# Reordering the first stage of a hybrid decoder layer: an earlier second chunk, eight buffers for modulation weights, squares summed by TensorE

## What is computed

```
mod = silu(c) @ w_ada + b_ada                      # c: one vector per sequence, 9 in all; w_ada: 1024 x 6144
sh1, sc1, gt1, sh2, sc2, gt2 = split(mod, 6)
h = rmsnorm(x, norm1_g) * (1.0 + sc1) + sh1        # rmsnorm: x * rsqrt(mean(x*x) + eps) * g
proj = h @ w_in                                    # then RG-LRU, mLSTM and pool groups, w_out, and the MLP
```

## Time and profile before

| what | value |
|---|---|
| median of 3 runs | 1172.3 us |
| the profiled execution | 1172.33 us |
| its span in the trace | 1170.5 us |
| PE busy | 1123.7 us, 96% of the span |
| DVE, ACT, POOL busy | 795.6, 470.4, 341.7 us |
| mean DMA rate over the span | 94 GB/s |
| start of `V:0` in the trace | 51.66 us |
| start of `V:5` in the trace | 93.79 us |

### The profile page before, as it was taken

One profiled execution on the slowest core, in us unless ns is written; L12 is line 12 of the kernel. 1 busy time (PEld: TensorE's weight loads), 2 busy tenths in 40 slices (PEclk: granted clock), 3 DMA queues, 4 the chain that ended last, 5 costly groups with the idle time before them and its releaser, 6 DMA issues.

```text
span 1170.5 us, 19691 instructions
## 1 busy us (share of the span) xinstructions
PE 1123.7 (96%) x7237; PEld 1075.4 (92%) x7237; DVE 795.6 (68%) x1327; ACT 470.4 (40%) x774; POOL 341.7 (29%) x273
## 2 busy tenths in 40 slices
PE   4899999999989999999999999999999999999997
PEld 2688888888978999899999999999999999999996
DVE  4472455489775434778678879778778787788546
ACT  5452355555456343642233332332432433433431
POOL 1133011201425357764022032122231231231352
PEclk9799999999989999999999999999999999999998
DMA  9812523566623822111111111202202102111104
GB/s 316 311 66 82 142 91 126 171 186 225 187 79 122 270 75 72 54 55 37 37 36 55 56 36 60 66 18 72 67 9 80 59 18 78 47 53 55 37 1 145
DMA packets 67846, 109.85 MB, mean 94 GB/s; under 512 B 6435, under 2 KB 42567, under 8 KB 67399
## 3 DMA queue, kind: packets, MB, share of 16 engines
q1 hardware_dynamic: 57574, 84.88, 21.9%
q10 hardware_dynamic: 10208, 24.12, 6.5%
HBM read 96.81 MB, written 12.18 MB: 93 GB/s over the span
## 4 chain that ended last, share of the span: by engine, by line
PE 81%; DVE 11%; ACT 3%; issue 1%; POOL 1%; DMA 1%; SPq 0%; ACTq 0%; POOLq 0%; DVEq 0%
PE D L2412 7%; PE D L2414 6%; PE D L2413 6%; PE D L2596 6%; PE D L2598 5%; PE D L2597 5%; PE X L2598 5%; PE X L2596 5%; PE X L2597 5%; PE X L2668 5%; PE X L2670 5%; PE X L2669 5%; PE D L2668 2%; PE D L2670 2%; PE D L2669 2%
## 5 line engine op out<-in xcount | busy, mean ns | idle before, releaser
L2412 PE MATMUL D<-H_hi,W_hi 128*128 128x344 f32 x472 | 159.1, 337 | 6.9 <-POOL H_lo L1086 6.1
L2414 PE MATMUL D<-H_hi,W_lo 128*128 128x344 f32 x472 | 152.1, 322 | 0.0
L2413 PE MATMUL D<-H_lo,W_hi 128*128 128x344 f32 x472 | 152.1, 322 | 0.0
L1086 POOL TENSOR_TENSOR Y_lo<-FU,Y_hi 128x344 fp32r<-128x344 f32 (+3 forms) x84 | 100.1, 1195 | 153.7 <-ACT Y_hi L1522 87.6
L1081 POOL TENSOR_TENSOR W_lo<-RAWW,W_hi 128x1024 fp32r<-128x1024 f32 x25 | 61.3, 2452 | 178.8 <-ACT W_hi L1235 178.5
L2412 PEld LDWEIGHTS D<-H_hi,W_hi 128*128 128x128 f32 x472 | 90.1, 191 | 17.7 <-issue 11.8
L1086 POOL TENSOR_TENSOR Y_lo<-EY,Y_hi 128x344 fp32r<-128x344 f32 (+1 forms) x24 | 38.3, 1597 | 216.3 <-ACT Y_hi L1522 144.5
L2413 PEld LDWEIGHTS D<-H_lo,W_hi 128*128 128x128 f32 x472 | 90.1, 191 | 0.6 <-issue 0.2
L2414 PEld LDWEIGHTS D<-H_hi,W_lo 128*128 128x128 f32 x472 | 89.8, 190 | 0.0
L2220 DVE SCALAR_TENSOR_TENSOR X<-X,MOD 128x344 f32<-128x344 f32 (+1 forms) x138 | 75.6, 566 | 9.3 <-PE X L2670 9.2
L2668 PE MATMUL X<-Y_hi,W_hi 128*128 128x344 f32 x252 | 80.7, 320 | 0.0
(11 more groups left out here) (417 smaller groups left out, 3434.8 us busy)
## 6 DMA issues: line engine op xcount, KB each, us to landing
RAWW<-in_W SPq DMA_DIRECT2D x76, 512.0 KB, 3.6
RAWW<-in_WADA ACTq DMA_DIRECT2D x28, 512.0 KB, 4.1
RAWW<-in_WADA SPq DMA_DIRECT2D x20, 512.0 KB, 6.5
RAWW<-in_W ACTq DMA_DIRECT2D x18, 512.0 KB, 3.7
X0T<-in_x SPq DMA_DIRECT2D x3, 1376.0 KB, 12.9
out_y<-OUTN SPq DMA_DIRECT2D x24, 172.0 KB
X<-in_x SPq DMA_DIRECT2D x8, 344.0 KB, 5.5
NM<-nm_d SPq DMA_DIRECT2D x8, 256.0 KB, 5.4
```

The costliest lines, as they stand in the source:

```text
L1086: nc.gpsimd.tensor_tensor(lo_v, fu_v, hi_v.bitcast(F32), ALU.subtract).then_inc(lo_ready, 1)
L2412: T.matmul(out, w_h, hi[:, kt, a:b], start=(kt == 0), stop=False)
L2413: T.matmul(out, w_h, lo[:, kt, a:b], start=False, stop=False)
L2414: one = T.matmul(out, w_l, hi[:, kt, a:b], start=False, stop=(kt == KT - 1))
```

## The change

Six things, all in the first stage:

- `x` chunk 1 is asked for behind the fourth piece (after `w0`) instead of behind the sixteenth, chunk 2 behind the sixteenth.
- The 16 starting pieces go to eight buffers: the four of `RAWW` and four spare places in memory that is free then (three where `WV_lo` will be, one in `MU`'s place). A piece waits for the use of the piece eight before it. Eight pieces leave the ring's numbering, so `R:20` becomes `R:12`, and so on.
- `MIX_ORDER` begins with the squares of chunk 0 instead of with pieces, and the squares and the norm of chunk 1 stand directly behind `N:0:0 N:0:1`.
- From there the two chunks go on together, row tile by row tile, with the units' products on chunk 1 between those on chunk 0. `DK:1:1` (unit 1 on chunk 1) stays whole and stands ahead of `V:0`.
- The squares of chunks 0 and 1 are no longer added by DVE. PE multiplies each square by the ones matrix and accumulates in the norm's bank: eight fp32 matmuls for a chunk instead of one. ACT waits for PE before it overwrites one of the two `SQ` tiles.
- The squares of chunk 2 are still added by DVE; they move from before `V:2` to between `V:0` and `V:1`, and `NS:2` to behind `V:1`.

```diff
-SP_AFTER = {5: ("w0",), 7: ("w1",), 15: ("wv", "x1"), 17: ("x2",), 18: ("w2",)}
+SPARE = 4
+SPARE_PIECES = [k for n, k in enumerate(ADA_EARLY) if n % (RAW + SPARE) >= RAW]
+SP_AFTER = {3: ("w0", "x1"), 5: ("w1",), 15: ("wv", "x2"), 17: ("w2",)}
 ...
-ADA:0:0 ADA:0:1 SQ:0:0 ADA:4:0 ADT:0 ADM:0 ADA:4:1 SQ:0:1 ADA:1:0 ADT:4 ADM:4 NS:0 ADA:1:1 W:0 N:0:0 N:0:1 ADA:5:0 ADT:1 ADM:1
-ADA:5:1 W:1 ADA:2:0 ADT:5 ADM:5 DK:0:0:0:2 N:0:2 N:0:3 ADA:2:1 DK:1:0:0:2 ADA:6:0 ADT:2 ADM:2 ADA:6:1 DK:0:0:2:4
-    ADA:3:0 ADT:6 ADM:6 N:0:4 N:0:5 DK:1:0:2:4 ADA:3:1 ADA:7:0 ADT:3 ADM:3 DK:0:0:4:6 ADA:7:1 ADT:7 ADM:7 N:0:6 N:0:7 DK:1:0:4:6
+SQ:0:0 ADA:0:0 SQ:0:1 NS:0 ADA:0:1 ADA:4:0 ADT:0 ADM:0 ADA:4:1 ADT:4 ADM:4 W:0 N:0:0 N:0:1
+SQ:1:0 SQ:1:1 ADA:1:0 DK:0:0:0:2 ADA:1:1 NS:1 ADA:5:0 ADT:1 ADM:1 W:1 ADA:5:1 DK:1:0:0:2 ADT:5 ADM:5 N:1:0 N:0:2 N:0:3 N:1:1
+ADA:2:0 ADA:2:1 DK:0:1:0:1 DK:0:0:2:3 ADA:6:0 ADT:2 ADM:2 DK:1:0:2:3 ADA:6:1 DK:0:0:3:4 DK:1:0:3:4 ADT:6 ADM:6 N:0:4 N:1:2 N:0:5 N:1:3
+DK:0:1:1:2 ADA:3:0 ADA:3:1 DK:0:1:2:3 ADA:7:0 DK:0:0:4:5 ADT:3 ADM:3 DK:1:0:4:5 ADA:7:1 DK:0:1:3:4 ADT:7 ADM:7 N:0:6 N:1:4 N:0:7 N:1:5 N:1:6 N:1:7
+DK:0:0:5:6 DK:1:0:5:6
 WV:0 DK:0:0:6:7
 ...
-D:0:0 SQ:1:0
-D:1:0 SQ:1:1 V:0 NS:1 ADA:8:0 N:1:0 N:1:1 V:1 N:1:2 N:1:3 DK:0:1:0:1
 ...
+WV:3 D:0:0 DK:0:1:5:6
+D:1:0 DK:0:1:6:7
+DK:0:1:7:8
+D:0:1 DK:1:1:0:8
+D:1:1 V:0 ADA:8:0 SQ:2:0 V:1 SQ:2:1 NS:2
+R:12 ADA:8:1 V:2 N:2:8 N:2:0 R:13 N:2:1 N:2:2 V:3 N:2:3 N:2:4 N:2:5 ADT:8 N:2:6 V:4 N:2:7 ADM:8 DK:0:2:0:8
 ...
+            def square_taken(n):
+
+                c, kt = n // KT, n % KT
+                if c >= N_PE_SQ:
+                    act.wait_ge(ss1_done, n - N_PE_SQ * KT + 1)
+                elif kt == KT - 1:
+                    wait_full(act, ("NS", c))
+                else:
+                    act.wait_ge(sq_summed, c * (KT - 1) + kt + 1)
 ...
+                    for kt in range(part * KT // 2, (part + 1) * KT // 2):
+                        n = c * KT + kt
+                        pe.wait_ge(sq_ready, n + 1)
+                        one = T.matmul(bank(key)[:, 0:CH], ONE[:], SQ[:, n % 2, :], start=(kt == 0), stop=(kt == KT - 1))
```

More of the change, by code:

```diff
@@ L54 @@
 ADA_START = (0, 4, 1, 5, 2, 6, 3, 7)
-ADA_FIRST = 2 * len(ADA_START)
+ADA_EARLY = [("ADA", i, h) for i in ADA_START for h in range(2)]
 N_MIX = 2 * LRU_T + 3 * ML_T + POOL_T
@@ L120 @@
 W:2 V:5
-D:0:2 R:22 DK:1:2:0:8
-ADA:9:0 ADA:9:1 R:23 V:6 V:7 W:3 V:8 R:25 ADT:9
+D:0:2 R:14 DK:1:2:0:8
+ADA:9:0 ADA:9:1 R:15 V:6 V:7 W:3 V:8 R:17 ADT:9
 D:1:2 ADM:9 ADA:10:0 G1 ADA:10:1
-D:2:0 ADT:10 R:24
-D:2:1 ADM:10 R:26 G2
-D:2:2 R:28 W:4 G3 ADA:11:0 R:27 R:29
+D:2:0 ADT:10 R:16
+D:2:1 ADM:10 R:18 G2
+D:2:2 R:20 W:4 G3 ADA:11:0 R:19 R:21
 D:3:0 ADA:11:1 G4
-D:3:1 R:31 ADT:11 LRUC:0
+D:3:1 R:23 ADT:11 LRUC:0
 D:3:2 ADM:11 W:5 ADA:12:0
-D:4:0 R:30 ADA:12:1 LRUG:0 R:32 LRUA:0
+D:4:0 R:22 ADA:12:1 LRUG:0 R:24 LRUA:0
@@ L131 @@
 D:4:1 LRUM:0
-D:4:2 R:34 W:6
-D:5:0 ADT:12 ADM:12 ADA:13:0 ADA:13:1 R:33 LRUC:1
+D:4:2 R:26 W:6
+D:5:0 ADT:12 ADM:12 ADA:13:0 ADA:13:1 R:25 LRUC:1
 D:5:1
-D:5:2 ADT:13 R:35 ADM:13 ADA:14:0 LRUG:1 ADA:14:1
-D:6:0 R:37 W:7 ADT:14 LRUA:1 R:36 R:38 ADM:14
+D:5:2 ADT:13 R:27 ADM:13 ADA:14:0 LRUG:1 ADA:14:1
+D:6:0 R:29 W:7 ADT:14 LRUA:1 R:28 R:30 ADM:14
 D:6:1 LRUM:1
-D:6:2 R:40 ADA:15:0
+D:6:2 R:32 ADA:15:0
 D:7:0
-D:7:1 W:8 ADA:15:1 LRUC:2 R:39
+D:7:1 W:8 ADA:15:1 LRUC:2 R:31
 D:7:2 ADT:15 LRUG:2 LRUA:2
-D:8:0 R:41 ADM:15 ADA:16:0 W:9
@@ L143 @@
-D:8:1 R:43
-D:8:2 R:42 ADA:16:1 R:44 W:10 LD:0 SMA TS TSD ADT:16 LRUM:2
+D:8:0 R:33 ADM:15 ADA:16:0 W:9
+D:8:1 R:35
+D:8:2 R:34 ADA:16:1 R:36 W:10 LD:0 SMA TS TSD ADT:16 LRUM:2
 D:9:0
-D:9:1 R:46 R:45 LD:1 ADM:16 EX:0 ADA:17:0 S:0 SX:0 ADA:17:1 W:11 AB:0 R:47
+D:9:1 R:38 R:37 LD:1 ADM:16 EX:0 ADA:17:0 S:0 SX:0 ADA:17:1 W:11 AB:0 R:39
 D:9:2 ADT:17 U:0 NU:0 HN:0 CN:0 ADM:17 HM:0 EX:1 ADA:18:0 SMK S:1 SX:1 SMB:0
@@ L173, in plan_mix @@
 def plan_mix():
-    raws = [("ADA", i, h) for i in ADA_START for h in range(2)]
+    raws = [k for k in ADA_EARLY if k not in SPARE_PIECES]
     pairs = [i for i in range(NPAIR) if i not in ADA_START]
     early, pairs = pairs[:2], pairs[2:]
-    raws += [("ADA", i, h) for i in early for h in range(2)]
+    early = [("ADA", i, h) for i in early for h in range(2)]
+    raws += early
     for u in range(3, N_MIX):
@@ L185, in plan_mix @@
         out.append((name, *(int(a) for a in args)))
-    return out, raws
+    return out, raws, ADA_EARLY + early
 AUX = ["X0", "X1", "X2", "X3", "X4"]
@@ L298, in build @@
     P_FF = P_MIX + P_NORM
-    assert len(raw_seq) == N_MIX - N_EARLY_W + NADA
+    assert len(raw_seq) == N_MIX + R0
     raw_seq += [("W", u) for u in range(N_MIX, N_MIX + RAW)]
     raw_at = {k: n for n, k in enumerate(raw_seq)}
-    ADA_ORDER = [k[1] for k in raw_seq if k[0] == "ADA" and k[2] == 0]
+    ADA_ORDER = list(ADA_START) + [k[1] for k in raw_seq if k[0] == "ADA" and k[2] == 0 and k[1] not in ADA_START]
     SHIFTED = ((1, 3, 5, 7, KT), (KT - 2, KT - 1, KT))
@@ L367, in build @@
         WV_lo = at("WV_lo", [P, KT, VCOLS], rX + KT * VCOLS * 4, F32R)
+        SPARE_RAW = [at(f"SPARE{r}", [P, KT * P], rX + KT * VCOLS * 4 + r * KT * P * 4 if r < SPARE - 1 else slot[15]) for r in range(SPARE)]
         VS = [at(f"VS{b}", [P, HEADS, HV], rX + 2 * KT * VCOLS * 4 + 1568 * b) for b in range(2)]
@@ L478, in build @@
         raw_in = [sem(f"raw{r}_in") for r in range(RAW)]
+        spare_in = [sem(f"spare{r}_in") for r in range(SPARE)]
         w_hi_ready, w_lo_ready = sem("w_hi_ready"), sem("w_lo_ready")
@@ L560, in load_raw, with used @@
                 e.dma_start(RAWW[:, n % RAW, :], I["W"][in_unit(u)]).then_inc(raw_in[n % RAW], 16)
[L562 to L564 removed]
+        def used(e, key):
             if key[0] == "W":
@@ L570, in raw_used @@
                 e.wait_ge(ada_half, ADA_ORDER.index(key[1]) + 1)
+        def raw_used(e, n):
+            used(e, raw_seq[n])
         def mod_ready(e):
@@ L809, in _ @@
             load_x(0)
[L810 to L813, removed]
+            for n, key in enumerate(sp_raws):
+                if key in SPARE_PIECES:
+                    k = SPARE_PIECES.index(key)
+                    if k >= SPARE:
+                        used(sp, SPARE_PIECES[k - SPARE])
+                    load_piece(sp, key, SPARE_RAW[k % SPARE][:], spare_in[k % SPARE])
+                else:
+                    if raw_at[key] >= RAW:
+                        raw_used(sp, raw_at[key] - RAW)
+                    load_raw(sp, raw_at[key])
                 for what in SP_AFTER.get(n, ()):
@@ L2422, in _ @@
                 k = s[0]
-                if k == "NS":
-                    sum_squares(s, s[1], ss1_done, (s[1] + 1) * KT)
+                if k == "SQ" and s[1] < N_PE_SQ:
+                    _, c, part = s
+                    key = ("NS", c)
+                    if part == 0:
+                        take(key)
+                    for kt in range(part * KT // 2, (part + 1) * KT // 2):
+                        n = c * KT + kt
+                        pe.wait_ge(sq_ready, n + 1)
+                        one = T.matmul(bank(key)[:, 0:CH], ONE[:], SQ[:, n % 2, :], start=(kt == 0), stop=(kt == KT - 1))
+                        if kt < KT - 1:
+                            one.then_inc(sq_summed, 1)
+                        else:
+                            done(one, key)
+                elif k == "NS" and s[1] >= N_PE_SQ:
+                    sum_squares(s, s[1], ss1_done, (s[1] + 1 - N_PE_SQ) * KT)
                 elif k == "ADA":
```

90 lines of the change are left out of this document (42 added, 48 removed).

## The result

The changed kernel takes 1193.6 us (median of 4 runs, 1191.78 to 1196.85) against 1172.59 for the kernel before in the same session (1172.24 to 1173.58). The ratio is 1.0177, 95% interval 1.0154 to 1.0200: 21 us slower. The prediction said slower, by 8.7 us, and 1181.0; the time lies outside its range of 1170 to 1186. The profiled execution took 1191.78 us, the shortest of the four, with a span of 1190.0 against 1170.5; so the traces differ by 19.5 us and the medians by 21.0.

A forecast was written before the change was run, and what follows sets the result against it. PE was taken as the bound, 96% busy. `V:5` at 101.1 plus 1.4 for the clock, against 93.79 before, gave 8.7 us more: 1181.0 us from 1172.33, range 1170 to 1186.

The forecast's parts named there:

- the walk to 43 us: First stage, queue by queue from the start until DVE starts `N:1:0`, put at 42.65 us against `N:0:6` at 44.58 before.
- rival *faster: Waits of 17.4 us in the first stage are covered: 1163.6 us if all, deciding from half; chance 0.19.
- I am wrong if: Signs: `N:1:0` starts below 36, PE isn't idle ahead of `SQ:1:0`, or the trace distance shrinks from `V:5` to the end.
- first batch: Unit 0 on chunk 1, from `N:1:0` at 42.65: 8.25 us, plus 1.4 for starting at half clock.
- `NS:2` to `V:5`: End of the walk: chunk 2's norm, pieces, `V` products and a `DK` of 3.8, from 82.8 to 101.1 us.
- until the rise some 4 us on, of which 0.45 fills the wait: +1.4: First batch starts at half clock, its `DK`s, piece and `ADT` costing 1.9 more, less 0.45 absorbed: 1.4 us.
- wait of 3 us ahead of `NS:2`: PE waits 3 us for DVE's second half of chunk 2's squares, which stands behind the copy of `V:1`.
- 8.25 us a batch: Each of the first two batches of chunk 1's pieces, from DVE's start through `ADM`, takes 8.25 us at full clock.
- 2.6 + 0.95: Head of each batch: 2.6 us from DVE's start until the first low part is there, 0.95 to the next.
- a bound of 0 to +2: Issue time of some 10 PE switches between a piece and a `DK`, left out of the walk: 0 to +2 us.
- every batch at half clock: Rival: waits of 2.3 and 2.0 us make batches two and three start low too, 1.5 to 2 each: 1184.5 us; chance 0.14.
- the distance should not have grown: Behind `V:5` both kernels have the same work left, so a shift there moves the end by about as much.

The follow-up runs named there:

- after_fill: Changed kernel with filler matmuls on PE, whose results nobody reads, ahead of its six long waits; 1191.99 us, ratio 1.0132.
- after_dve_order_fill: Changed kernel with all squares added by DVE, fillers on PE, chunk 2's squares ahead of `V:0` and the `D:0:0` copy moved earlier; 1175.54 us, ratio 1.0011.
- before_first_fill: Kernel before with eight buffers, chunk 0's squares first (on DVE), chunk 1 asked for behind the value weights, and fillers in an unused bank; 1169.66 us, ratio 0.9967.
- after_order: Changed kernel with chunk 2's squares ahead of `V:0` and the `D:0:0` copy ahead of the third value-weight part, no fillers; 1194.4 us, ratio 1.0168.
- after_dve_squares: Changed kernel with the squares of chunks 0 and 1 added by DVE again; 1193.2 us, ratio 1.0153.

## Why the prediction was right in sign and short in size

**Right: the walk to 43 us.** First sum 9.15 (said 9.75), first reciprocal ended 20.5 (21.2), PE idle 4.14 (4.4) ahead of chunk 1's first sum at 25.58 (26.45), second reciprocal ended 38.95 (39.15), 3.07 idle (3) on `W_lo`, `N:1:0` at 43.55 (42.65). Nothing hid PE's sums, the early chunk was no help, and eight buffers gave nothing that a time shows. Chunk 0's first four sums took 4.63 us and chunk 1's eight 7.80, half of them at half clock, about as walked (4.75 and 7.25). The rival *faster* asked that half of 17.4 us of waits be covered; all stood. "I am wrong if" named three signs, and none of them came.

**Short: 8.8 us up to `V:5`.** Between the same landmarks, in us; the last column, with the clock held, tells the clock's part from the rest:

| stretch | walked | after | after_fill |
|---|---|---|---|
| start to `N:1:0` | 42.65 | 43.55 | 43.06 |
| first batch | 9.65, 1.4 of it for the clock | 11.86 | 8.85 |
| second batch | 8.25 | 9.59 | 9.57 |
| third batch's start to `V:0` | 11.45 | 13.48 | 13.53 |
| `V:0` to `NS:2` | 12.2 | 12.61 | 12.60 |
| `NS:2` to `V:5` | 18.3 | 20.24 | 18.80 |

- *"until the rise some 4 us on, of which 0.45 fills the wait: +1.4"* is the term that failed first. The first product of the batch (46.44) still took 0.40, the full-clock price; the clock fell behind it and stayed at half from 47.4 to 54.3, 7 us. It cost 3.0 (11.86 less 8.85), not 1.4.
- *`NS:2` to `V:5` was walked at full clock.* The wait of 3 us ahead of `NS:2` was right (3.17), but half clock came behind it, from 91.9 to 95, and cost 1.4. With the 1.6 that the first batch's clock cost beyond its 1.4, the clock is 3.0 of the 8.8.
- *"8.25 us a batch"* was too short at any clock: 8.85 and 9.57. In the second, PE's first product comes 3.86 behind DVE's start, where the walk had 2.6 + 0.95, and the work behind it takes 5.7 for 4.7. The walk left out the time to switch between a piece and a `DK`, which it had as a bound of 0 to +2; the batches filled 1.9 of it.
- *The copy of `D:0:0`* was missed, in the 2.0 of the third stretch. It stands behind the four parts of `WV` on ACT (71.11 to 74.11), so PE's next unit has no bank until it is done: `[1.13 <-issue]` at 74.64. It was in the list to be read. With the clock held the wait is 1.43, and `V:0` comes 1.5 us earlier without it. It also swallowed the half clock of 67.9 to 71.3: that stretch is as long with the clock held.

The rest, some 2.4 us, is in parts of half a us; 0.5 of it, ahead of `N:1:0`, is the clock too, and no run takes the others apart.

The rival *every batch at half clock* looks right by its number and isn't. It put 3.5 us on top of the 1.4, 4.9 in all, and the fillers gave back 4.9 at G1 (5.8 against the other execution). But it laid the 3.5 on the second and third batch, and there the fillers gave back nothing (9.57 for 9.59, 13.53 for 13.48). The 4.9 are 3.0 in the first batch, 1.4 behind `NS:2` and 0.5 ahead of `N:1:0`: the match is luck.

The Trainium skill, "TensorE: Matmul & The Clock Gate", section "HAM oscillation — how this bites in real kernels", says that bursts between waits restart low each time. The traces of the changed kernel agree in part. Behind the waits that end near 26, 41, 47, 68 and 91 the clock was low in both executions. But the burst began low in both only near 26; near 47 and 91 its first product took the full-clock price in both (0.40; 0.84 and 0.85), and the clock fell one or two us into it. Behind the wait of 2.81 ahead of the second batch it stayed full in both.

**From `V:5` to the end** the distance should not have grown; it grew by 2.0. The mLSTM stretch is 76.0 to 76.6 in the three traces in which its windows all stand at 1.00 (before, after_dve_order_fill, before_first_fill), and 77.7 to 83.5 in the other eleven, each of which has one to three windows of 20 us at 0.83 to 0.97. Stretch and clock go together in all fourteen; the fillers of the first stage don't decide it (83.2 and 80.9 with them, 76.1 and 76.0 too). I made no run that holds the clock in that stretch; what sets it off, and whether the changed kernel meets it more often or was unlucky in its profiles, stays open. What lies behind the stretch takes 861.9 to 864.4 us in the fourteen, so a difference of up to 2.5 us between two traces can also come from there.

**The change as a whole.** With the clock held the ladder at G1 is 130.2 (after), 125.2 (squares back on DVE), 120.1 (two waits taken out), against 113.4 for the old list, eight buffers and only chunk 0's squares moved. So of the 17.5, 5 are two waits of the new order and 10 are the clock and the sums together. Split as measured these are 5 and 5; with the 1.8 us of the first fillers moved over, 6.7 and 3.2. Taking all three out leaves 2.5 over the kernel before, which itself has a low clock in this stage (0.50 from 26 to 32 and from 48 to 56 us). This holds for the traces; the medians fall by 18 us over the same ladder, but in steps of another size. The remaining 6.7 between 120.1 and 113.4 were not taken apart: the row-by-row order with its batches, and the early chunk, are both in it.

## What to carry to other kernels

In a list that each engine walks in order, price a reordering by walking it to the first point where both versions have done the same work, and look in every engine's queue for the copy that frees a bank, not only for the operand. Check a match of numbers stretch by stretch: here a rival's 4.9 us came out exactly, in other places than it said. Where PE waits a few us several times, bound the clock at every wait and not only at the first: it took over a quarter of the loss here, and the gain of two fixed waits was invisible until fillers held it. A part that shows no wait in one order (an early transfer) can cost 3 us in another; so undo parts with the clock held, one at a time, and with the same fillers.

## What the runs showed of the hardware

- The granted clock isn't a function of the program alone. In two executions of the changed kernel the product behind one wait of 2.6 us took 0.57 (67.89) and 0.40 (68.76). In after_order the clock stayed at 0.50 through windows in which PE was busy 8.5 and 9.6 of 10 us, and in after_dve_squares through four windows of 2 us (54 to 62) in which PE was busy all the time.
- The clock column isn't to be trusted at the start. In the ten kernels that begin with a piece it takes 1.08 us near 10 us, the half-clock price, in windows that say 1.00; in after_dve_squares the column says 1.00 over products at the half-clock price up to 46 us. There only the lengths of the instructions tell.
- An fp32 product of 128x344 against the ones matrix takes 0.58 us at full clock and about 1.2 back to back at half (4.63 for four); 128 columns take 0.24 and 0.46 (9 fillers in 2.17 us, 10 in 4.64).
- Fillers with `start=True` in other columns of a bank whose sum was still open changed that sum; in an unused bank they touched nothing. The Trainium skill, "PSUM — Partial Sum Buffer", section "The four PSUM rules", says that such a start clears the accumulation marks of the whole bank, so that the open sum is overwritten and not added to. The runs agree: with such fillers the first output was off by a relative 0.18 in all three kernels.
